# Sixteen free bytes behind each 2 KiB row in the rings of split weights of a two-block transformer kernel

## What is computed

```python
# first block
z = rms_norm(x, norm_mix_w) @ w_in            # 2048 x 11264: scan, band attention, gates
merged = gate_a * (y_a @ w_branch_a) + gate_b * (y_b @ w_branch_b)   # 1024 x 2048 each
h = x + merged @ w_out                        # 2048 x 2048
u = rms_norm(h, norm_mlp_w)
h = h + square(relu(u @ w_up)) @ w_down       # 2048 x 8192 and 8192 x 2048
x = rms_norm(h, norm_final_w)
# second block, with 16 meta tokens put in front
proj = rms_norm(concat(meta, x), pre_norm_g) @ w_in_2                # 2048 x 6656
y = concat(ya, yb) @ w_out_2                  # two attentions; 2048 x 2048
out = x + rms_norm(y, post_norm_g)
```

## Time and profile before

| what | value |
|---|---|
| time, median of 2 runs | 1894.94 us |
| the two runs | 1893.66 and 1896.22 us |
| span of the profiled execution | 1893.3 us |
| TensorE busy, weight loads busy | 99%, 92% |
| VectorE, ScalarE, GpSimd busy | 58%, 47%, 8% |
| granted TensorE clock | full in nearly the whole span |
| HBM read | 342.44 MB, 182 GB/s over the span |

### The profile page before, as it was taken

How to read it: one execution, slowest core, us unless ns; L and a number is a source line. 1 busy time by engine, 2 the same in 40 slices (tenths; PEclk the granted TensorE clock), 3 DMA queues, 4 the chain that set the end, 5 groups by cost and what they waited for, 6 DMA issues and landing times.

```text
span 1893.3 us, 33876 instructions
## 1 busy us (share of the span) xinstructions
PE 1879.6 (99%) x13432; PEld 1743.7 (92%) x13432; DVE 1101.4 (58%) x1270; ACT 889.3 (47%) x1171; POOL 143.6 (8%) x122
## 2 busy tenths in 40 slices
PE   9999999999999999999999999999999999999998
PEld 9989998999999889988998899899889999899986
DVE  6556766667655555545445445445565556767664
ACT  6544444455544445443444344334454355664543
POOL 2001322411001100000010000000010000000000
PEclk9999999999999999999999999999999999999999
DMA  8566565566565656656665665566556655354454
GB/s 270 184 181 177 181 179 178 165 200 180 168 231 191 214 186 179 194 198 192 196 192 193 194 191 194 194 190 190 189 185 181 179 170 150 105 147 144 156 190 143
DMA packets 176434, 346.47 MB, mean 183 GB/s; under 512 B 10976, under 2 KB 11184, under 8 KB 175776
## 3 DMA queue, kind: packets, MB, share of 16 engines
q1 hardware_dynamic: 174176, 337.76, 57.2%
q0 software_dynamic: 2128, 6.82, 1.4%
HBM read 342.44 MB, written 2.10 MB: 182 GB/s over the span
## 4 chain that ended last, share of the span: by engine, by line
PE 97%; DVE 1%; ACT 0%; DMA 0%; issue 0%; SPq 0%; DVEq 0%; ACTq 0%
PE ps L446 58%; PE ps L458 33%; PE ps L548 1%; PE ps L781 1%; DVE wlo L1301 1%; PE ps L771 1%; PE ps L748 1%; PE ps L791 0%; DMA raw<-in_w_in_dram 0%; ACT whi L899 0%; PE ps L476 0%; PE ps L759 0%; PE ps L599 0%; PE ps L591 0%; DVE xlo L1323 0%; PE ps L610 0%
## 5 line engine op out<-in xcount | busy, mean ns | idle before, releaser
L1301 DVE TENSOR_TENSOR wlo<-raw,whi 128x1024 fp32r<-128x1024 f32 x631 | 796.5, 1268 | 698.1 <-ACT whi L899 697.1
L899 ACT ACTIVATE whi<-raw 128x1024 fp32r<-128x1024 f32 x631 | 664.5, 1058 | 886.3 <-PE ps L446 551.5
L446 PE MATMUL ps<-xhi,whi 128*128 128x256 f32 (+1 forms) x1904 | 542.2, 285 | 0.4 <-DVE wlo L1301 0.3
L446 PE MATMUL ps<-xhi,wlo 128*128 128x256 f32 (+1 forms) x1904 | 531.3, 279 | 0.0
L446 PE MATMUL ps<-xlo,whi 128*128 128x256 f32 x1664 | 462.5, 278 | 0.0
L446 PEld LDWEIGHTS ps<-xhi,whi 128*128 128x128 f32 x1904 | 359.1, 189 | 9.3 <-issue 6.7
L446 PEld LDWEIGHTS ps<-xhi,wlo 128*128 128x128 f32 x1904 | 357.8, 188 | 0.0
L446 PEld LDWEIGHTS ps<-xlo,whi 128*128 128x128 f32 x1664 | 313.4, 188 | 1.5 <-issue 0.7
L446 PE MATMUL ps<-x2hi,whi 128*128 128x256 f32 x1024 | 282.8, 276 | 0.0
L446 PE MATMUL ps<-x2hi,wlo 128*128 128x256 f32 x1024 | 282.7, 276 | 0.0
L446 PE MATMUL ps<-x2lo,whi 128*128 128x256 f32 x1024 | 282.7, 276 | 0.0
(11 more groups left out here) (373 smaller groups left out, 2370.6 us busy)
## 6 DMA issues: line engine op xcount, KB each, us to landing
raw<-in_w_in_dram SPq DMA_DIRECT2D x279, 512.0 KB, 3.8
raw<-in_w_up_dram SPq DMA_DIRECT2D x128, 512.0 KB, 3.7
raw<-in_w_down_dram SPq DMA_DIRECT2D x128, 512.0 KB, 3.7
raw<-in_w_out_dram SPq DMA_DIRECT2D x64, 512.0 KB, 3.8
raw<-in_w_branch_a_dram SPq DMA_DIRECT2D x16, 512.0 KB, 4.9
raw<-in_w_branch_b_dram SPq DMA_DIRECT2D x16, 512.0 KB, 3.8
x_nat<-in_x_dram SPq DMA_DIRECT2D x4, 512.0 KB, 7.4
rel<-in_rel_turned_dram POOLq DMA_DIRECT2D x8, 256.0 KB, 4.3
```

Source lines behind the costliest of these rows:

```text
L446: ins = mm(outs[b], w[:, k % SLOTS, j, cols], v, start=start, stop=last and j == CK - 1 and i == 2, skip_group_check=True)
L899: f(whi[:, k % SLOTS], raw[:, k % SLOTS], ACT.Copy).then_inc(whi_ready, 1)
L1301: tt(wlo[:, k % SLOTS], raw[:, k % SLOTS], whi[:, k % SLOTS], ALU.subtract).then_inc(wlo_ready, 1)
```

## The change

The rings of `whi` and `wlo` get rows of 516 numbers instead of 512 (2064 bytes instead of 2048). The names `whi` and `wlo` now stand for the first 512 numbers of each row. Nothing that reads or writes them is changed in the text of the kernel, and `raw` stays as it was.

```diff
 SLOTS = 4
+CW_ROW = CW + 4
 X_PLACE = 48
...
         raw = sb("raw", [P, SLOTS, CK, CW])
-        whi = sb("whi", [P, SLOTS, CK, CW], F32R)
-        wlo = sb("wlo", [P, SLOTS, CK, CW], F32R)
+        whi_rows = sb("whi", [P, SLOTS, CK, CW_ROW], F32R)
+        wlo_rows = sb("wlo", [P, SLOTS, CK, CW_ROW], F32R)
+        whi, wlo = whi_rows[:, :, :, 0:CW], wlo_rows[:, :, :, 0:CW]
         sb("x_place", [P, X_PLACE])
```

## The result

The changed kernel took 1936.31 us in the median of 2 runs (1936.22 to 1936.4), against 1894.94 us (1893.66 to 1896.22). The ratio is 1.0218, 95% interval [1.0193, 1.0243], so the change made the kernel about 2% slower. The profiled execution has a span of 1934.3 us, 41.0 us more than before.

The account below looks back on a forecast made before the run. The prediction took TensorE, busy 99% of the span, to bound the kernel. It added 15 us for the 256-column matmuls and zero elsewhere to the 1893.3 us span, giving 1908, or 1910 us as median, range 1872 to 1960.

Parts of the forecast that it names:

- L446 above 118 ns: Sign of being wrong, on the 256-column matmul line in long runs: it would mean clearly slower.
- What bounds the kernel: Whole kernel: TensorE is busy 99% of the span, so only what a matmul costs can move the time.
- ScalarE, VectorE, DMA and the tensors behind the rings at nothing: Ring writes and reads, loads and later tensors: no change, operations staying near 1058 and 1268 ns.
- The inference from the two paces: 256-column matmuls at 113.3 and 117.8 ns: moving and stationary reads disturb each other more in one step than another.
- half of the matmuls of each pace change to the other: 256-column matmuls: 3550 slow down and 850 speed up by 4.5 ns each, +12 us.
- the sixteen places: 256-column form: weights against tokens get sixteen relative places instead of one, spread over what the streams can do.
- The second reckoning: 256-column form: one settling of 24 ns at each of 736 ring row changes, +18 us.
- The 512-column form at zero: Matmuls with rings as moving operand: no change, within bounds of 39 us less and 24 us more.
- rival "faster": TensorE reads: changing distance spreads collisions, shrinking slow pace and excess, 109 us in all; 1840 us with half; chance 0.13.
- rival "clearly slower": All matmul forms: old place near the best, most others worse; 32 + 4 + 24 = +60 us, 1955 us; chance 0.20.
- The rule of the Trainium skill: TensorE: two independent read ports, weight loading takes no read bandwidth from the running matmul; no change, 1895 us.
- the floor: Matmul cost estimated as half the plain float32 time of 428.75 ns: 214.4 ns for 512 columns, 107.2 for 256.

Follow-up runs that it names:

- moved_256: Against the kernel before: rows of 512 kept, everything behind the rings 256 bytes further on; 1894.09 us.
- all_32: Against the kernel before: 32 free bytes ahead of both rings, so rings and tokens move together; 1895.05 us.
- const_32: Against the kernel before: rows of 512, both rings 32 bytes later against the tokens, constant; 1939.5 us.
- yt_64: Against the kernel before: rings unmoved, only the four token tensors of the last product moved to the weights' place within 256; 1892.85 us.
- same_distance: Against the kernel before: both rings with rows of 516, row r of each at the same place within 256; 1941.93 us.
- lo_16: Against the kernel before: rows of 512, `wlo` alone 16 bytes later, constant; 1930.6 us.
- const_16: Against the kernel before: rows of 512, both rings 16 bytes later against the tokens, constant; 1941.23 us.
- const_192: Against the kernel before: rows of 512, both rings 192 bytes later, weights and tokens at one place within 256; 1938.33 us.

## Why the prediction was wrong

The result of 1936 us lies inside the range of 1872 to 1960, but the forecast was 15 us more than before, and 41 us more were measured, 2.7 times as much. The direction was right and the size was not. One of the prediction's own signs of being wrong was met: L446 above 118 ns (118.4). Point by point:

- *What bounds the kernel* held. The 41 us are in the pace of TensorE's matmuls (36.2 + 6.0 - 1.2).
- *ScalarE, VectorE, DMA and the tensors behind the rings at nothing* held (1059 and 1266 ns; moved_256 at 1894 us).
- *The inference from the two paces*, that the two operands disturb each other by their relative place, held as far as the runs go: all_32 and const_32 show it for the rings, yt_64 for the tokens of the 512-column form. That the disturbance lies in two reads of SBUF made at once is still an inference, because no run separates the weight load from the matmul.
- *The step that failed* is "half of the matmuls of each pace change to the other". It took the sixteen places as spread evenly over the two paces. In fact nearly all that were seen are bad. In same_distance the offsets of 16 to 112 bytes take 118.2 to 119.7 ns each. Of the upper eight only 128 and 192 were tried by themselves in both rings. In the changed kernel itself the rows 1 to 7 take 117.5 to 119.2 ns, and only row 0 comes near the fast pace, in its second half. The constant offsets of 4, 16, 32, 64 and 192 bytes have 117 to 120 ns in every long run, and moving the weights of one matmul in three (lo_16) is enough to lose the fast pace. Instead of 3550 matmuls at +4.5 ns, about 7100 went up by 5.0, and almost none of the 1700 slow ones came down. By these estimated counts that is 36 us, and by the whole trace 34, where the prediction had 12 and then took 15.
- *The second reckoning*, one settling of 24 ns per row, gave +18 us by a mechanism that is secondary. Settling exists (row 0 above), but const_16 has no settling at all and costs more, and row 0 of same_distance comes out of a slow row and is fast at once. That the two reckonings, +12 and +18 us, lay close together was no support for either.
- *The 512-column form at zero* failed as well. It was excused by "no second pace has shown". It has at least two (228.9 and 233.3), it went to 231.1, and 2688 x 2.2 = 5.9 us came from that. The other reason given, that the weight load runs in only a part of the matmul (less than half of the time, as the rival "faster" says), was a wrong reading. In a stretch of the kernel before in which only L458 runs, TensorE's weight loads are busy for 32.81 of 40 us, or 82% (window in us, its length, PE busy, PEld busy, granted clock, DMA share, GB/s):
```profile
1000.00:1040.00 40.00, 40.00 (x176) 32.81 (x176) 1.00 0.60 202
```
- *The rival "clearly slower"* had the mechanism: the old distance is near the best, and most others hold the slow pace or a worse one. Its term for 256 columns, 32 us, was nearly right (34 measured). Those for 272 and 512 columns, 4 and 24 us, were too large (2 and 6), so its 1955 us came out 19 us too high. Its reason, that a moving place takes the settling away, is the *step* theory and fell as the main cause. The hint in the trace was named there and got a chance of 0.20 only: at the one distance that the trace shows, long undisturbed runs were fast, so that distance was a good one, and leaving a good one is more likely to cost than to gain.
- *The rule of the Trainium skill* ("TensorE: Matmul & The Clock Gate", step-by-step part on how a matmul is issued), that loading the next weights takes no read bandwidth from the running matmul, would have left 1895 us in every kernel of the table. The runs contradict it as a rule on time, for the float32r operands of this kernel. With the same instructions, the 256-column pace is 113.3 or 117.8 ns at the old distance and 120.0 ns throughout at another (const_192).
- *The rival "faster"* fell for 256 columns. No place went below 113.3 ns. For 512 columns one place went below the pace of before (226.7 against 228.9). At 2.4 GHz these best paces are 272 and 544 cycles, both 6% over one per column. So no place that was tried comes near the floor of 107.2 and 214.4 ns on which the gain of this rival was reckoned, and what makes up this 6% stays open.

## What to carry to other kernels

In a kernel that is bound by back-to-back float32r matmuls, look at the place of the stationary operand against the moving one within 256 bytes. In this kernel it was worth up to 3% (1894 to 1948 us on multiples of 16 bytes), and no instruction count shows it. Divide an undisturbed run of matmuls by its number and compare such runs: two paces of one form are a warning, and a change that moves any tensor then has to be followed down to the addresses modulo 256. One steady pace is no all-clear, as const_16 holds a bad place at one pace. Here spreading the rows over many places averaged over mostly bad ones. What held the fast pace was one good distance, found by trial and kept by rows that are whole multiples of 256 bytes.

## What the runs showed that was not expected

- One and the same code with the same distances has two steady paces for hundreds of matmuls. The first long run took 117.8 ns per matmul in the kernel before and 113.4 in moved_256 (29.94 us for 264). all_32 and yt_64, with the same distances there, have 117.8 again.
- `wlo` may be 128 bytes from its place at no loss for 256 columns (113.4 ns), but 16 or 64 bytes take the mean of the group to 117.8 or 118.2.
- The two forms want different distances: at the same place within 256, 512 columns take 226.7 ns and 256 columns 120.0; 64 bytes apart, 228.9 and 113.3.
- A row that starts 4 bytes off makes the 512-column matmul 239.9 ns instead of 228.9.
